# A fifth Strassen-Winograd pair per chunk in the "up" stage of two SwiGLU layers, one of its weight sums moved to an accumulating DMA and the gate product moved to GpSimd

## What is computed

```python
D_MODEL, SEQ, D_FF = 2048, 256, 5632

def swiglu(x, wg, wu, wd):
    return (jax.nn.silu(x @ wg) * (x @ wu)) @ wd

f = swiglu(rmsnorm(h, ffn1_pre_g[l]), ffn1_wg[l], ffn1_wu[l], ffn1_wd[l])
h = h + FFN_RES_WEIGHT * rmsnorm(f, ffn1_post_g[l])
...
f = swiglu(rmsnorm(h, ffn2_pre_g[l]), ffn2_wg[l], ffn2_wu[l], ffn2_wd[l])
h = h + FFN_RES_WEIGHT * rmsnorm(f, ffn2_post_g[l])
```

## Time and profile before

| | |
|---|---|
| median of three runs | 2065.04 us (2064.78 to 2065.18) |
| profiled execution | span 2063.8 us from the first to the last instruction; 26172 instructions |
| TensorE busy | 2050.5 us, 99% |
| VectorE busy | 1813.9 us, 88% |
| ScalarE busy | 1152.8 us, 56% |
| GpSimd busy | 27.7 us, 1% |
| traffic | 409.51 MB, 198 GB/s |

### The profile page before, as it was taken

The page is one execution under the profiler, slowest core; times in us unless marked ns, Lnnn a source line. Parts: engine busy times, 40 slices in busy tenths (PEclk is TensorE's granted clock), DMA queues, the critical chain, the costliest instruction groups (busy, mean ns, idle before and its releaser), DMA issues.

```text
span 2063.8 us, 26172 instructions
## 1 busy us (share of the span) xinstructions
PE 2050.5 (99%) x9238; PEld 1694.8 (82%) x9238; DVE 1813.9 (88%) x2227; ACT 1152.8 (56%) x1292; POOL 27.7 (1%) x54
## 2 busy tenths in 40 slices
PE   9999999999999999999999999999999999999998
PEld 8888888888888788888788888888888888888886
DVE  7999999999888858998687566879999999999797
ACT  6565665566555554444466444565656565665463
POOL 0000000000000000100000000000000000000000
PEclk9999999999999999999999999999999999999999
DMA  8666656655666666776555566566666666646564
GB/s 327 222 207 203 202 187 212 211 164 177 201 194 205 187 186 192 208 202 183 178 169 181 181 191 213 183 233 201 198 205 208 198 203 201 206 143 207 198 208 163
DMA packets 211996, 409.51 MB, mean 198 GB/s; under 512 B 15113, under 2 KB 15377, under 8 KB 211520
## 3 DMA queue, kind: packets, MB, share of 16 engines
q1 hardware_dynamic: 209904, 401.26, 60.4%
q0 software_dynamic: 1856, 7.01, 1.5%
q10 hardware_dynamic: 144, 0.04, 0.0%
HBM read 406.14 MB, written 2.11 MB: 198 GB/s over the span
## 4 chain that ended last, share of the span: by engine, by line
PE 98%; DVE 1%; ACT 0%; issue 0%; DMA 0%; POOL 0%; DVEq 0%; SPq 0%; ACTq 0%; POOLq 0%
PE banks L1731 96%; PE banks L1781 2%; DVE wlo L1059 0%; DVE res L1114 0%; DMA raw<-in_ffn_wg_dram 0%; DVE h_lo L1349 0%; ACT act_hi L579 0%; DVE act_lo L1127 0%; ACT h_hi L767 0%; POOL stat L476 0%; ACT comb L683 0%; DVE comb L1083 0%; ACT junk L644 0%; ACT whi L564 0%; PE banks L2028 0%
## 5 line engine op out<-in xcount | busy, mean ns | idle before, releaser
L564 ACT ACTIVATE whi<-raw 128x1024 fp32r<-128x1024 f32 x579 | 597.8, 1052 | 490.2 <-PE banks L1731 298.3
L1059 DVE TENSOR_TENSOR wlo<-raw,whi 128x1024 fp32r<-128x1024 f32 x580 | 690.6, 1217 | 154.4 <-ACT whi L564 152.2
L1731 PE MATMUL banks<-whi,act_hi 128*128 128x512 f32 x1568 | 507.8, 395 | 0.7 <-DVE wlo L1059 0.7
L1731 PE MATMUL banks<-whi,act_lo 128*128 128x512 f32 x1568 | 498.2, 389 | 0.0
L1731 PE MATMUL banks<-wlo,act_hi 128*128 128x512 f32 x1568 | 485.2, 389 | 0.3 <-DVE wlo L1059 0.3
L1731 PEld LDWEIGHTS banks<-whi,act_lo 128*128 128x128 f32 x1568 | 294.3, 188 | 62.1
L1731 PEld LDWEIGHTS banks<-wlo,act_hi 128*128 128x128 f32 x1568 | 294.3, 188 | 62.0 <-DVE wlo L1059 0.7
L1731 PEld LDWEIGHTS banks<-whi,act_hi 128*128 128x128 f32 x1568 | 291.1, 188 | 62.5 <-issue 4.7
L564 ACT ACTIVATE whi<-raw_deep 128x1024 fp32r<-128x1024 f32 x176 | 183.0, 1054 | 172.4 <-DVE raw_deep L1259 156.3
L1059 DVE TENSOR_TENSOR wlo<-raw_deep,whi 128x1024 fp32r<-128x1024 f32 x176 | 207.8, 1220 | 7.0 <-ACT whi L564 6.9
L1731 PE MATMUL banks<-whi,h_hi 128*128 128x512 f32 x536 | 172.9, 390 | 0.5 <-ACT whi L564 0.5
(11 more groups left out here) (305 smaller groups left out, 2392.6 us busy)
## 6 DMA issues: line engine op xcount, KB each, us to landing
raw<-in_ffn_wd_dram SPq DMA_DIRECT2D x176, 512.0 KB, 4.7
raw<-in_w_in_dram SPq DMA_DIRECT2D x160, 512.0 KB, 3.6
raw<-in_ffn_wg_dram SPq DMA_DIRECT2D x88, 512.0 KB, 3.7
raw_deep<-in_ffn_wg_dram SPq DMA_DIRECT2D x88, 512.0 KB, 3.7
raw<-in_ffn_wu_dram SPq DMA_DIRECT2D x88, 512.0 KB, 4.7
raw_deep<-in_ffn_wu_dram SPq DMA_DIRECT2D x88, 512.0 KB, 4.5
raw<-in_w_out_dram SPq DMA_DIRECT2D x32, 512.0 KB, 4.1
raw<-in_w_pw_dram SPq DMA_DIRECT2D x16, 512.0 KB, 4.0
```

The source lines that it names most:

```text
L564: nc.scalar.activation(whi[:, j % RING, 0:kts * width], src[:, 0:kts * width], ACT.Copy).then_inc(hi_ready, 1)
L1059: nc.vector.tensor_tensor(wlo[:, j % RING, 0:n], raw_slot(j, deep)[0][:, 0:n], whi[:, j % RING, 0:n], ALU.subtract).then_inc(lo_ready, 1)
L1731: return nc.tensor.matmul(o, a, b, **kw)
```

## The change

It has four parts.

1. `SEVEN` is (1, 2, 3, 5, 6): five pairs of each of the 2 x 10 summed chunks are done with seven products, not four. Each such pair now needs its weight sums and their conversions.
2. For the up stage the sum b12 + b22 is no longer made by VectorE. GpSimd issues a DMA that reads the b22 half of slab 2q+1 from HBM once more (128 x 512, 256 KB) and adds it onto the b12 half in its slot (`accum_op=ALU.add`). ScalarE (before it converts slab 2q+1) and VectorE (before its sums) wait for it, on `pair_added`.
3. The three other weight sums are made in two VectorE instructions: R = b11 - (b12 + b22) (512 columns), then Z = R + b21 and P = R + b22 in one instruction of 2 x 512 columns (`sums_of_lower_rows`). Signs of an activation sum and in `combine` are turned to match. In the down stage VectorE makes b12 + b22 itself, first, and then these two; the product with `w_out` keeps its code, but for what it shares with the rest.
4. `hidden(c)` of the up stage moves to GpSimd as one product of 128 x 1024. The row factor is applied ahead of it by two ScalarE copies with a scale, behind SiLU. The last hidden product of each layer stays on VectorE.

```diff
-SEVEN = (1, 3, 5, 6)
+SEVEN = (1, 2, 3, 5, 6)
...
-P_SUM, R_SUM, Z_SUM = range(3)
+Z_SUM, P_SUM, R_SUM = range(3)
...
+            def pair_sums(f):
+
+                def hidden(c):
+
+                    pool.wait_ge(silu_ready, SUMMED * f + c)
+                    pool.wait_ge(h_psum, UP_CHUNKS * f + c)
+                    nc.gpsimd.tensor_tensor(nat[:], comb[:, C12:C12 + TT, :], comb[:, C11:C11 + TT, :], ALU.mult).then_inc(hidden_ready, 1)
+
+                def one(c, group):
+                    first = isinstance(c, int) and c == 1
+                    for q in SEVEN:
+                        if q == SEVEN[-2] and not first:
+                            hidden(c - 1)
+                        slab, full = raw_slot(2 * q + 1, True)
+                        pool.wait_ge(full, 16 * loads_in_up(f, c, 2 * q + 1))
+                        pool.dma_start(slab[:, 0:CW], rows(w_up[f][1])[:, 2 * q + 1, bass.ts(c, CW)],
+                                       accum_op=ALU.add).then_inc(added(f, c, q)[0], 16)
+
+                summed_chunks(pool.Fori, one)
...
                     for t in range(TT):
-                        ins = nc.scalar.activation(comb[:, C11 + t, :], comb[:, C11 + t, :], ACT.Silu, scale=stat[:, RSTD + t:RSTD + t + 1])
+                        nc.scalar.activation(comb[:, C11 + t, :], comb[:, C11 + t, :], ACT.Silu, scale=stat[:, RSTD + t:RSTD + t + 1])
+                    for t in range(TT):
+                        ins = nc.scalar.activation(comb[:, C12 + t, :], comb[:, C12 + t, :], ACT.Copy, scale=stat[:, RSTD + t:RSTD + t + 1])
                     ins.then_inc(silu_ready, 1)
...
                         hi_at(2 * q)
                         if q in SEVEN:
-                            act.wait_ge(wsum_ready, 4 * seven + 3)
+                            act.wait_ge(*added(f, c, q))
                         hi_at(2 * q + 1)
...
+                def sums_of_lower_rows(n, deep):
+
+                    s = n % DEEP if deep else n % RING
+                    two = raw[:, s:s + 2, CW:2 * CW] if s < RING else raw_deep[:, s - RING:s - RING + 2, CW:2 * CW]
+                    return nc.vector.tensor_tensor(wsum[:, Z_SUM:P_SUM + 1, :], wsum[:, R_SUM:R_SUM + 1, :].to_broadcast([P, 2, CW]),
+                                                   two, ALU.add)
...
-                    nc.vector.tensor_tensor(wsum[:, P_SUM, :], b11, b12, ALU.add).then_inc(wsum_ready, 1)
+                    nc.vector.tensor_tensor(b12, b12, b22, ALU.add).then_inc(wsum_ready, 1)
                     dve.wait_ge(wsum_ready, 4 * seven + 1)
-                    nc.vector.tensor_tensor(wsum[:, R_SUM, :], wsum[:, P_SUM, :], b22, ALU.add).then_inc(wsum_ready, 1)
-                    nc.vector.tensor_tensor(b12, b12, b22, ALU.add).then_inc(wsum_ready, 1)
+                    nc.vector.tensor_tensor(wsum[:, R_SUM, :], b11, b12, ALU.subtract).then_inc(wsum_ready, 1)
                     dve.wait_ge(wsum_ready, 4 * seven + 2)
-                    nc.vector.tensor_tensor(wsum[:, Z_SUM, :], wsum[:, R_SUM, :], b21, ALU.add).then_inc(wsum_ready, 1)
+                    sums_of_lower_rows(n - 1, deep).then_inc(wsum_ready, 2)
+
+                def up_weight_sums(c, q, seven, opens):
+
+                    if not opens:
+                        dve.wait_ge(wsumlo_ready, seven)
...
+                    dve.wait_ge(*added(f, c, q))
+                    nc.vector.tensor_tensor(wsum[:, R_SUM, :], b11, b12q, ALU.subtract).then_inc(wsum_ready, 2)
+                    dve.wait_ge(wsum_ready, 4 * seven + 2)
+                    sums_of_lower_rows(2 * q, True).then_inc(wsum_ready, 2)
...
-                        if q == 6 and not first:
-                            hidden(c - 1)
```

More of the change, by code:

```diff
@@ L266, in build @@
             sem("wsum_ready"), sem("wsumhi_ready"), sem("wsumlo_ready"), sem("wsum_used"))
+        pair_added = [sem(f"pair_added{i}") for i in range(RING)]
         outer_copied, combined, silu_ready, hidden_ready = (
@@ L345, in summed_chunks, with added @@
             one(SUMMED, 0)
+        def added(f, c, q):
+            i = (2 * q + 1) % DEEP // 2
+            per_chunk = sum((2 * n + 1) % DEEP // 2 == i for n in SEVEN)
+            so_far = sum((2 * n + 1) % DEEP // 2 == i for n in SEVEN if n <= q)
+            return pair_added[i], 16 * (per_chunk * SUMMED * f + per_chunk * (c - 1) + so_far)
         def raw_slot(j, deep):
@@ L481, in _ @@
             root(1, rstd)
-            pool.wait_ge(mm_done, UP_SLABS)
+            def pair_sums(f):
[13 more added lines that the diff above has]
+                summed_chunks(pool.Fori, one)
+            pair_sums(0)
             load_gpost(f1_post)
@@ L541, in _ @@
             root(7, rstd)
+            pair_sums(1)
             root(8, rpost[0])
@@ L736, in quad @@
                     if q in SEVEN_OF[half]:
-                        act.wait_ge(wsum_ready, 4 * seven + 3)
+                        act.wait_ge(wsum_ready, 4 * seven + 1)
                     hi_at(n + 1)
@@ L1219, in act_sums @@
                     link(nc.vector.tensor_tensor(asum[:, i, S5, :], a21, a22, ALU.subtract))
-                    nc.vector.tensor_tensor(asum[:, i, S7, :], a11, a21, ALU.subtract)
+                    nc.vector.tensor_tensor(asum[:, i, S7, :], a21, a11, ALU.subtract)
                     link(nc.vector.tensor_tensor(asum[:, i, S6, :], asum[:, i, S5, :], a11, ALU.subtract))
@@ L1240, in hidden @@
                     dve.wait_ge(h_psum, UP_CHUNKS * f + c)
[L1241 to L1244, removed]
+                    nc.vector.tensor_tensor(nat[:], comb[:, C12:C12 + TT, :], comb[:, C11:C11 + TT, :], ALU.mult).then_inc(hidden_ready, 1)
+                def sums_of_lower_rows(n, deep):
[3 more added lines that the diff above has]
+                                                   two, ALU.add)
                 def weight_sums(seven, loads, j, opens, deep=False):
@@ L1274, in combine @@
                     dve.wait_ge(combined, combined_count(f, c, 2))
-                    nc.vector.tensor_tensor(comb[:, C12:C22 + 1, :], comb[:, C22:C22 + 1, :].to_broadcast([P, 2, CW]),
-                                            comb[:, C12:C11:-1, :], ALU.subtract).then_inc(combined, 2)
+                    nc.vector.tensor_tensor(comb[:, C12:C22 + 1, :], comb[:, C12:C11:-1, :],
+                                            comb[:, C22:C22 + 1, :].to_broadcast([P, 2, CW]), ALU.subtract).then_inc(combined, 2)
                 def combine_last(c, group, done):
@@ L1291, in summed @@
                         if q in SEVEN:
-                            weight_sums(seven, loads_in_up(f, c, 2 * q), 2 * q, first and f == 0 and q == SEVEN[0], deep=True)
+                            up_weight_sums(c, q, seven, first and f == 0 and q == SEVEN[0])
                         if q == SEVEN[0] and not first:
@@ L1323, in hidden_sums @@
                     link(nc.vector.tensor_tensor(down_sum[:, i, S5, :], a21, a22, ALU.subtract))
-                    nc.vector.tensor_tensor(down_sum[:, i, S7, :], a11, a21, ALU.subtract)
+                    nc.vector.tensor_tensor(down_sum[:, i, S7, :], a21, a11, ALU.subtract)
                     link(nc.vector.tensor_tensor(down_sum[:, i, S6, :], down_sum[:, i, S5, :], a11, ALU.subtract))
@@ L1332, in extra_sums @@
                     a11, a12, a21, a22 = (extra_full[:, e, k, t * P:(t + 1) * P] for t in range(TT) for k in range(2))
-                    nc.vector.tensor_tensor(extra_sum[:, e, S7, :], a11, a21, ALU.subtract)
+                    nc.vector.tensor_tensor(extra_sum[:, e, S7, :], a21, a11, ALU.subtract)
                     link(nc.vector.tensor_tensor(extra_sum[:, e, S5, :], a21, a22, ALU.subtract))
```

6 lines of the change are left out of this document (added).

## The result

The changed kernel takes **2219.13 us**, the median of four runs (2217.71 to 2220.49), against 2065.11 for the kernel before beside it: a ratio of 1.0745 (95% interval 1.0732 to 1.0758). The profiled execution's span is 2217.3 us, 153.5 more than before.

The account below looks back on a forecast made before the run. TensorE sets the time, with VectorE nearly full. Chunks of 48.8 us, 7.1 more, in 18 chunks give +128; less 7 for the lead and 1 for chunks c = 1, +120: 2185 us, range 2120 to 2270.

Parts of the forecast that it names:

- VectorE from pair 3's sums to pair 5: Up-stage chunk: VectorE converts slabs 6 to 9 and makes a low part, reaching pair 5's sums after 6.2 us.
- `silu_ready`: ScalarE's path from the end of pair 3's sums through SiLU and two new copies to this semaphore: 5.8 us.
- X: GpSimd's hidden product of 128 x 1024: between 1.2 and 5.0 us, taken as 2.4.
- Y: Pair 5's accumulating DMA, from issue to landing: between 3.2 and 8.3 us, taken as 5.6.
- The stall: VectorE's wait at pair 5 for its DMA: X + Y - 0.3 = 7.7 us, in 18 chunks.
- VectorE's own work: VectorE's time per summed chunk with five pairs, without the stall: 41.1 us.
- TensorE has 7 us a chunk in hand: If TensorE's clock should fall in the longer gaps, its idle time of some 7 us a chunk is spare.
- The lead of VectorE pays 3.5 us of each layer's first stall: First stall of each layer: VectorE has slab 10's low part 3.5 us early, twice, -7 us.
- c = 1 gains 0.6 each; the down stage's entry costs nothing: The two chunks c = 1, without a hidden product on GpSimd: -0.6 us each; the down stage: nothing.
- slow accumulates: Rival, 14%: reading the destination makes Y 12 us, pair 1's accumulate also late, 2331 us; decided from Y = 10.3.
- All hidden, 2053: Rival, 6%: VectorE finds pair 5's sum in place, chunks take 41.1 us, 2053 us in all.
- VectorE and GpSimd shut each other out: Rival, 8%: GpSimd's product can't begin during VectorE's two-input operation, starting at 6.2 instead of 5.8: +7, 2192 us.

Follow-up runs that it names:

- the first run: Changed kernel with GpSimd's gate product moved behind the accumulating DMA of pair 6, so that no DMA stands behind it: 2120.99 us.
- the second run: Changed kernel with the gate product back on VectorE as one instruction behind pair 6's conversions, GpSimd only issuing the accumulating DMAs: 2096.55 us.
- the filled gap: Changed kernel with 16 more TensorE products, repeating one of pair 5, per chunk from the second on, where TensorE waits for VectorE: 2208.22 us.

## Why the prediction was right, and which terms were off

It said 2185 us, slower, range 2120 to 2270; measured 2219.13. The forecast mechanism, pair 5's DMA behind the product in GpSimd's list and VectorE waiting for it, is what the trace shows, and moving one thing at a time confirmed it: without the product in front of pair 5's DMA the stall is gone (2121), with SiLU sooner the chunk shrinks by what SiLU gains, and the lower clock is gone (2166). By its own steps, per chunk:

- *VectorE from pair 3's sums to pair 5:* forecast 6.2, measured 6.29. *`silu_ready`:* 5.8, measured 6.04. *X:* 2.4 by the middle of its bounds, measured 2.43.
- *Y:* 5.6 from `bgate`'s median; measured 4.52 (4.14 to 5.32) to landing, 4.63 to VectorE's start with the 0.1 of the semaphore. Mis-sized by 1 us, towards `bgate`'s least. The fit of the Trainium skill (DMA: Bandwidth & Descriptors, "Anatomy of one DMA — SWDGE (gpsimd) path") gives 2.6, further off on the other side. The stall: 7.7 forecast, 6.83 measured: -0.9 x 18 = -16 us.
- *VectorE's own work:* 41.1 forecast. Measured: a chunk of the first run, 44.17, less the lock's 2.21 is 42.0 in the first layer, and the same comes out of the changed kernel's 48.8 without the clock less 6.8 of stall. A pair's sums take 322.26 - 320.33 = 1.93, not 1.87 (5 times); the gap in front of a neighbouring pair is 0.17, not 0.12; and the 0.27 in front of `combine` was taken out but is still there. 0.2 is not attributed. In the second layer waits of 0.2 to 0.3 us in front of L1308, on VectorE's own `wsum_lo`, make it 0.5 longer (43.20 against 42.73 in the second run): +0.9 x 9 + 1.4 x 9 = +21.
- *"TensorE has 7 us a chunk in hand" if its clock should fall:* wrong as put. TensorE's idle time (4.2 to 5.3 us at pair 5, not 7) stands before the slow stretch, not behind it, and the slow products hold `wsum_hi` for longer, on which ScalarE and then VectorE wait: +11 us by the filled gap.
- *The lead of VectorE pays 3.5 us of each layer's first stall:* wrong. Nine chunks cost 70.8 us and the eight distances from product to product, 49.56 in mean, give 8 x 7.87 = 63.0; the first one costs 7.8, no less than the others. TensorE already waits for VectorE at pairs 2 and 3 of chunk c = 1, as two rows of its timeline show. There is no lead left: +7.

```profile
63.42 0.73 PE L1778 MATMUL banks<-wlo,act_hi 128*128 128x512 f32 x2 [0.95 <-DVE wlo L1090]
...
69.47 0.74 PE L1778 MATMUL banks<-wlo,act_hi 128*128 128x512 f32 x2 [1.00 <-DVE wlo L1090]
```

- *c = 1 gains 0.6 each; the down stage's entry costs nothing:* measured +1.8 and +2.8, and +1.0 twice (ScalarE's two more copies in front of the last hidden product): +8 together.

120 - 16 + 21 + 11 + 7 + 8 = 151, of 153.5 in the trace. That the chunk came out so close is in part luck. Two errors of 0.9 us cancelled: the filled-gap run, in which the clock plays no part, has chunks of 48.8 us in the first layer, the number forecast, from 42.0 and 6.8 instead of 41.1 and 7.7. The misses left, the second layer's waits, the clock, the lead and the chunks c = 1, all made the kernel slower, which is why 2219 lies above 2185.

Of the rivals, *slow accumulates* is out: pair 5's took 5.3 at most, and the slowest of all hundred 8.7, where the rival needed 10.3. *All hidden, 2053* could not have been had: back to back, without even the wait in front of `combine`, VectorE's work is 42.73 - 1.14 = 41.6 us in the first layer and 42.1 in the second, where 41.1 was assumed: beside the 41.69 of before there is no gain in it. Taking the lock (18 x 2.2 = 40 us) out of the first run leaves 2081; that is worked out, not run. *VectorE and GpSimd shut each other out* was right as a mechanism and small in this kernel, as forecast, only because VectorE stands idle during the product: the product began 0.25 us before the end of a conversion and took 2.52, against 2.39 in the run with SiLU sooner. Wherever VectorE is at work the lock costs 1.4 to 2.2 us a chunk. It makes up 40 of the 56 us that are left when only the order is mended; the rest is mostly the fifth pair's.

So of the 154 us, undone in this order: 98 go with the product's place in front of pair 5's DMA (11 of them the clock; more, but for the lock that the new place brings), 24 with the product back on VectorE, 29 with the fifth pair, for which VectorE has no room, and 2, the copies at the down stage, stay. Another order shares them out otherwise: with the stall in place the fifth pair is worth 73.

## What to carry to other kernels

An idle engine's list is still a list: before a long operation goes into it, ask what stands behind it there and who waits for that. If the operation must go, put it behind the last transfer that someone needs soon.

Work moved from VectorE to GpSimd is not off VectorE if VectorE has operations with two SBUF inputs at that time: here 2.2 us of lock replaced 1.14 us of work. Look for it in durations by form, not among the waits.

Where one engine hands its results on through a single tile, its lead ends there: two chunks of different make don't share their spare time.

When two engines are full, count the second one's instructions from start to start with every small wait left in: the 0.9 to 1.4 us a chunk that were missed here are more than the 0.68 that the fifth pair gives TensorE.

## What the runs showed of the hardware that was not expected

- The lock between GpSimd and VectorE counts as busy time of the instruction that is held: 0.69 became 2.90 us on VectorE, 1.40 became 2.01 on GpSimd.
- An accumulating DMA of 256 KB from GpSimd's queue takes no longer than a plain one here: the hundred of the changed kernel landed after 4.1 to 8.7 us, median 5.5, where `bgate`'s eight took 4.2, 5.6 and 8.3 (least, median, most) in the kernel before. Pair 5's, with no slab load issued in the 7 us behind it, landed after 4.5 in mean. The issues of the changed kernel (count, KB each, median us to landing) answer to the earlier trace rows:

```profile
raw_deep<-in_ffn_wu_dram POOLq DMA_DIRECT2D x60, 256.0 KB, 5.8
```

- An issue of such a DMA occupies GpSimd for 0.85 to 1.20 us, 0.87 in the median.
- Behind a gap of 4.2 us TensorE's products stood at the lower clock level for 5.7 us (0.43 us apart in place of 0.23), though it was busy throughout; with the gap filled the clock stayed at 0.999. Shorter gaps do it too: in the run with all else as changed but four pairs the 18 gaps are 2.2 to 2.6 us long, and 14 of them are followed by a stretch at the lower level, most of 3 to 3.5 us. What makes the stretch short or long, and what spared four gaps, is not settled by these runs.
- In the second layer VectorE waits 0.2 to 0.3 us, three times a chunk, for its own earlier `wsum_lo`, at instructions that in the first layer go without a wait. Why is open.
